# Causal pooling as banded TensorE products, and the decay levels spread over the tiles of the input projection

## The reference, cut to what matters

```python
def multiscale_pool(u, pool_w, pool_scale):
    c = jnp.cumsum(u32, axis=1)
    for g, w in enumerate(POOL_WINDOWS):          # 2, 4, 8, 16
        means.append((cg - lag) / cnt)            # trailing mean over w positions
    pooled = jnp.stack(means, axis=2) - u32
    y = jnp.einsum('bsgc,gcd->bsgd', pooled.astype(u.dtype), pool_w)
    return y.reshape(B, S, D_POOL) * pool_scale

def step(state, inp):                             # hgrn2_recurrence, one chunk
    b = jnp.cumsum(g_c, axis=2)
    o_inter = jnp.einsum('bhtd,bhdv->bhtv', q_c * jnp.exp(b), state)
    scores = jnp.einsum('bhtd,bhsd,bhtsd->bhts', q_c, k_c, decay)
    o_intra = jnp.einsum('bhts,bhsv->bhtv', scores, v_c)
    new_state = jnp.exp(b_last) * state + jnp.einsum('bhsd,bhsv->bhdv', k_dec, v_c)
```

## Time and profile before

| what | value |
|---|---|
| median of three executions | 2828.55 us |
| the profiled execution: its own time | 2831.76 us |
| the profiled execution: its span | 2830.0 us |
| PE busy | 2630.8 us, 93% |
| DVE busy | 1367.0 us, 48% |
| ACT busy | 727.9 us, 26% |
| POOL busy | 685.3 us, 24% |
| mean granted TensorE clock | 0.958 |

### The profile page before, as it was taken

How to read it: one execution, slowest core, us unless ns; L and a number is a source line. 1 busy time by engine, 2 the same in 40 slices (tenths; PEclk the granted TensorE clock), 3 DMA queues, 4 the chain that set the end, 5 groups by cost and what they waited for, 6 DMA issues and landing times. The chain is left out here.

```text
span 2830.0 us, 36447 instructions
## 1 busy us (share of the span) xinstructions
PE 2630.8 (93%) x13232; PEld 2086.7 (74%) x13232; DVE 1367.0 (48%) x2271; ACT 727.9 (26%) x1465; POOL 685.3 (24%) x422
## 2 busy tenths in 40 slices
PE   7989888989879999997799999899999987999997
PEld 4867756867648888876678888788888765788886
DVE  4356834367653334467653333533344575633344
ACT  2135621156431110042431110211110424311101
POOL 1000031000223331117243331233311163433311
PEclk9998989979989999999899999999999997999999
DMA  5310013300122333221122333133332220223332
GB/s 193 97 45 1 2 60 126 96 1 2 38 89 92 94 102 102 78 84 58 39 81 90 96 108 102 56 97 96 99 103 88 75 67 31 79 93 96 103 103 80
DMA packets 57268, 222.22 MB, mean 79 GB/s; under 512 B 6664, under 2 KB 7816, under 8 KB 56768
## 3 DMA queue, kind: packets, MB, share of 16 engines
q1 hardware_dynamic: 56000, 214.01, 23.7%
q10 hardware_dynamic: 1152, 6.68, 0.6%
HBM read 218.51 MB, written 2.15 MB: 78 GB/s over the span
## 5 line engine op out<-in xcount | busy, mean ns | idle before, releaser
L214 PE MATMUL bank<-xh,two_hi 128*128 128x512 f32 x1856 | 741.5, 400 | 37.7 <-ACT xh L1173 33.7
L215 PE MATMUL bank<-xh,two_lo 128*128 128x512 f32 x1856 | 737.8, 398 | 0.0
L217 PE MATMUL bank<-xl,two_hi 128*128 128x512 f32 x1856 | 727.0, 395 | 0.0
L167 DVE CAST two_hi<-two_raw 128x1024 fp32r<-128x1024 f32 (+1 forms) x292 | 228.3, 782 | 952.7 <-PE bank L217 950.7
L214 PEld LDWEIGHTS bank<-xh,two_hi 128*128 128x128 f32 x1856 | 352.5, 190 | 129.3 <-issue 36.6
L215 PEld LDWEIGHTS bank<-xh,two_lo 128*128 128x128 f32 x1856 | 352.8, 190 | 82.0 <-issue 0.5
L217 PEld LDWEIGHTS bank<-xl,two_hi 128*128 128x128 f32 x1856 | 351.0, 189 | 82.7
L169 DVE TENSOR_TENSOR two_lo<-two_raw,two_hi 128x1024 fp32r<-128x1024 f32 (+1 forms) x292 | 395.5, 1355 | 10.0
L1395 POOL TENSOR_TENSOR up_hm<-up_sg,up_hm 128x512 f32<-128x512 f32 x88 | 197.9, 2249 | 581.2 <-ACT up_hm L1377 581.2
L214 PE MATMUL bank<-hh,two_hi 128*128 128x512 f32 x704 | 276.3, 392 | 0.0
L217 PE MATMUL bank<-hl,two_hi 128*128 128x512 f32 x704 | 274.1, 389 | 0.0
(11 more groups left out here) (314 smaller groups left out, 3185.6 us busy)
## 6 DMA issues: line engine op xcount, KB each, us to landing
two_raw<-in_up SPq DMA_DIRECT2D x180, 512.0 KB, 3.6
two_raw<-in_down SPq DMA_DIRECT2D x64, 704.0 KB, 4.0
one_raw<-in_w_in SPq DMA_DIRECT2D x52, 512.0 KB, 3.6
two_raw<-in_w_in SPq DMA_DIRECT2D x40, 512.0 KB, 3.6
one_raw<-in_w_out SPq DMA_DIRECT2D x16, 512.0 KB, 3.6
two_raw<-in_w_out SPq DMA_DIRECT2D x16, 512.0 KB, 3.7
w<-in_w ACTq DMA_DIRECT2D x2, 2048.0 KB, 10.6
x<-in_x SPq DMA_DIRECT2D x1, 2048.0 KB, 8.3
```

Source lines behind the costliest of these rows:

```text
L167: v.tensor_copy(st.hi[:, h, 0:w], st.raw[:, r, 0:w]).then_inc(st.hi_made, 1)
L214: pe.matmul(out[:], wh, xh[:, kx, :], start=start, stop=False)
L215: pe.matmul(out[:], wl, xh[:, kx, :], start=False, stop=False)
L217: return pe.matmul(out[:], wh, xl[:, kx, :], start=False, stop=stop)
```

## The change

In the mixers the pooling leaves POOL. For each chunk of 128 tokens PE multiplies u by the pooling weights (`pool_weights`, 16 products of 128 columns), ACT copies the results to SBUF, and PE multiplies them by constant banded matrices `kb` that hold the window means minus one (`pool_steps`: per window four products of 128 columns and three of 16 columns for what spills over from the chunk before). `kb` is loaded anew in each layer by a DMA that the ACT queue issues at tile 8, 128 rows of 4352 bytes. ACT writes `xh` of the pooling straight from PSUM, DVE writes its `xl`.

DVE takes over from POOL the key product and the query product; the keys' decay is made by ACT in 16 activations. The decay chain, the level work, the value and key transposes, five of the six masked levels and the pooling's weight product are placed among the tiles of the projection. `LINE` is doubled from 32 to 64 numbers. Core of the diff:

```diff
-LINE = 32
+LINE = 64
...
+    MASKED_LEVELS = (2, 3, None, 4, 5, 6)
...
             if i == 8:
-                a.wait_ge(s["e3"], 1)
...
+                a.dma_start(kb[:], kit.d["kb"]).then_inc(s["steps"], 16)
+                a.wait_ge(s["b_made"], HH * NT)
+                for b in range(HH * NT):
+                    c = slice(b * P, (b + 1) * P)
+                    a.activation(kd[:, c], bb[:, c], ACT.Exp, scale=-1.0, bias=bb[:, b * P + P - 1:b * P + P]
+                                 ).then_inc(s["ke_exp"], 1)
+                a.activation(el[:], bb[:, P - 1:W:P], ACT.Exp).then_inc(s["ke_exp"], 1)
+                level_exps(0)
...
             if i == 17:
-                level_exps(3)
...
+                level_exps(6)
+                a.activation(qe, bb[:], ACT.Exp).then_inc(s["qe_exp"], 1)
+                a.wait_ge(s["z_mm"], NT)
+                for n in range(NT):
+                    a.activation(zt[:, n, :], bank[n][:], ACT.Copy).then_inc(s["z_kept"], 1)
...
+        for c in range(HH):
+            a.wait_ge(s["p_mm"], c + 1)
+            a.activation(kit.xh[:, c, :], bank[6 + c % 2][:], ACT.Copy, scale=kit.s2[:, Q_PS + c:Q_PS + c + 1]
+                         ).then_inc(s["hi_made"], 1)
...
     def vector(v):
...
-            if i == 10:
+            if i in (6, 7):
                 v.wait_ge(s["a_made"], 1)
-                for h in range(HH):
+                for h in ((0, 1) if i == 6 else (2, 3)):
...
+            if i == 19:
+                v.wait_ge(s["qe_exp"], 1)
+                v.tensor_tensor(qe, qe, q, ALU.mult).then_inc(s["qe_made"], 1)
+                accumulate(4)
+        accumulate(5)
...
+        for c in range(HH):
+            v.wait_ge(s["hi_made"], c + 1)
+            v.scalar_tensor_tensor(kit.xl[:, c, :], bank[6 + c % 2][:], kit.s2[:, Q_PS + c:Q_PS + c + 1],
+                                   kit.xh[:, c, :].bitcast(F32), ALU.mult, ALU.subtract).then_inc(s["lo_made"], 1)
...
     def tensor(pe):
...
+        for i in range(D_V, N_IN2):
             dense(i)
+            if i == 11:
+                top_level(0)
+            if i == 12:
+                top_level(1)
+                turn_values(0)
+                turn_values(1)
+            if i == 13:
+                turn_values(2)
+                turn_values(3)
+            if i == 14:
+                masked_level(0)
+            if i == 15:
+                masked_level(1)
+            if i == 16:
+                masked_level(2)
+                turn_keys()
+            if i == 17:
+                masked_level(3)
+                pool_weights()
+            if i == 18:
+                masked_level(4)
+        masked_level(5)
+
+        pe.wait_ge(s["z_kept"], NT)
         for n in range(NT - 1):
             for h in range(HH):
...
+        pe.wait_ge(s["steps"], 16)
+        pe.wait_ge(s["out_taken"], 2 + N_IN2)
+        for c in range(HH):
+            if c >= 2:
+                pe.wait_ge(s["lo_made"], c - 1)
+            pool_steps(c)
...
     def gpsimd(g):
         apply_gpsimd(g, kit, s)
-        g.wait_ge(s["b_made"], HH * NT)
         g.wait_ge(s["v_turned"], NT)
...
         g.memset(at[:, 0:2, :, :], 0.0).then_inc(s["zeroed"], 1)
         g.memset(at[:, 2:4, :, :], 0.0).then_inc(s["zeroed"], 1)
```

More of the change, by code:

```diff
@@ L1539, in mixers @@
     dense_banks = bank[6:8]
[L1540 to L1546, removed]
+    s = kit.sems("mix", DENSE + APPLY_SEMS + (
+        "chain_v", "abs_f", "exp_f", "ln_f", "ls_made", "km_made", "k_made", "a_made", "m_made", "lb_in", "lb_act", "lb_made",
+        "e2", "e3", "e4", "b_made", "sub_made", "exp_made", "top_mm", "ke_exp", "lv_made", "lev_mm", "acc_made", "at_made",
+        "v_turned", "v_kept", "qe_exp", "qe_made", "kd_made", "k_turned", "k_kept", "kv_mm", "st_made", "o_mm", "o_kept",
+        "osq_made", "o_summed", "oln_made", "orstd_made", "y_made", "g_made", "z_mm", "z_kept", "p_mm", "hi_made",
+        "lo_made", "ylo_made", "zeroed", "steps"))
     q = p2[:, D_Q:D_Q + HH, :].rearrange("p h t -> p (h t)")
@@ L1639, in scalar @@
[L1639 to L1647, removed]
@@ new lines, in scalar @@
+            if i == 16:
+                a.wait_ge(s["k_turned"], NT - 1)
+                for n in range(NT - 1):
+                    a.activation(kr[:, n, :, :], bank[n][:].rearrange("p (h c) -> p h c", h=HH), ACT.Copy
+                                 ).then_inc(s["k_kept"], 1)
+            if i == 17:
+                level_exps(6)
[3 more added lines that the diff above has]
+                    a.activation(zt[:, n, :], bank[n][:], ACT.Copy).then_inc(s["z_kept"], 1)
@@ L1843, in top_level, with masked_level @@
                 mm.then_inc(s["top_mm"], 1)
-        def masked_level(i):
-            if i < len(MASKED) - 1:
-                pe.wait_ge(s["lv_made"], 2 * (i + 3))
-            if i >= 2:
-                pe.wait_ge(s["acc_made"], 2 * i - 3)
+        def masked_level(j):
+            i = MASKED_LEVELS[j]
+            if i is not None:
+                pe.wait_ge(s["lv_made"], 2 * i + 2)
+            if j < 2:
+                pe.wait_ge(s["v_kept"], NT)
+            else:
+                pe.wait_ge(s["acc_made"], max(1, 2 * (j - 2)))
             for n in range(NT):
@@ new lines, in pool_weights, with pool_steps @@
+        def pool_weights():
+            pe.wait_ge(s["k_kept"], NT - 1)
+            pe.wait_ge(s["out_taken"], 2 + D_U + HH)
+            for n in range(NT):
+                for c in range(HH):
+                    mm = pe.matmul(bank[n][:, c * P:(c + 1) * P], p2[:, D_U + c, n * P:(n + 1) * P],
+                                   kit.s2[:, Q_PW + c * P:Q_PW + (c + 1) * P], start=True, stop=True)
+                mm.then_inc(s["z_mm"], 1)
+        def pool_steps(c):
+            out = bank[6 + c % 2]
+            for n in range(NT):
+                first = FIRST_STEP if n == 0 else INNER_STEP
+                mm = pe.matmul(out[:, n * P:(n + 1) * P], zt[:, n, c * P:(c + 1) * P], kb[:, c, first:first + P],
+                               start=True, stop=n == 0)
+                if n:
+                    mm = pe.matmul(out[:, n * P:n * P + PADT], zt[:, n - 1, c * P:(c + 1) * P],
+                                   kb[:, c, SPILL_STEP:SPILL_STEP + PADT], start=False, stop=True)
+            mm.then_inc(s["p_mm"], 1)
@@ L1879, in tensor @@
-        for i in range(D_U + 1, D_G):
-            dense(i)
-        pe.wait_ge(s["v_kept"], NT)
-        top_level(0)
-        dense(D_G)
-        dense(D_G + 1)
-        top_level(1)
-        dense(D_G + 2)
-        dense(D_G + 3)
-        for c in range(HH):
-            pool_product(c)
-        pe.wait_ge(s["p_kept"], HH)
-        masked_level(0)
-        masked_level(1)
-        pe.wait_ge(s["kd_made"], 1)
-        pe.wait_ge(s["out_taken"], 2 + N_IN2)
-        pe.wait_ge(s["at_made"], 3 * NT)
+        dense_products(pe, st, s["out_taken"], l, "w_in_2", DC, kit.xh, kit.xl, dense_banks, first=D_Q, last=D_V)
```

266 lines of the change are left out of this document (121 added, 145 removed).

## The result

Median of six executions each: 2828.88 us before (2825.17 to 2831.14), 2749.25 us after (2740.12 to 2758.69), ratio 0.9721 [0.9699, 0.9742], which is 79.6 us less. The forecast was 2785.0 in a range from 2742 to 2806. The direction was right and the range held the time, but the likeliest value was 36 us too high; the forecast's own range, 2775 to 2797, did not hold it either. The wider range did because its lower end was rival 1, and the result lies 7 us above that rival's 2742, which had a chance of 0.18.

The account below looks back on a forecast made before the run. PE was taken to bound the kernel, with losses in the mixer tails. Per layer 62.0 - 26.8 - 13.4 = 21.8 us, twice 43.6, padding nothing: 2828.55 - 43.6 = 2785 us; range 2742 to 2806, its own 2775 to 2797.

Parts of the forecast that it names:

- rival 1: Padding helps because weights and activations then lie alike in 128-byte halves: 2742 us, chance 0.18.
- What bounded the kernel: PE, busy in 93% of the span; the mixer tails of 62.0 and 61.9 us were where time could be saved.
- Work between tiles: Five masked levels, key transposes and pooling weight products added among projection tiles: 13.4 us a layer at full clock.
- Is anything late: DVE, ACT and the `kb` load meet PE's waits among the tiles; tightest is tile 8's split, 0.6 us to spare.
- sign of being wrong: PE waiting for `two_lo` or "issue" between tiles, or tile intervals far from the mixers moved by over 0.05 us.
- The new tail: Tile 19 to the first output-projection product: 26.8 us, bounds 20.5 to 30, with PE idle 6 us for DVE.
- the restart: PE's loss to the low clock behind its wait for DVE in the tail, taken as 2.3 us.
- Sum of the rearrangement: Old tail less new tail and work between tiles: 21.8 us saved a layer, 43.6 in both.
- The padding: LINE 64 moves tiles behind `eps` by 128 bytes against `xh`; taken as no effect, though bounded at -43 us.
- Rival 2: Padding hurts because the slow half itself costs and `hh` and stationary tiles move into it: 2853 us, chance 0.09.
- Rival 3: Masked levels among tiles stall through "issue" gaps or a late DVE, 9 us a layer: 2803 us, chance 0.15.
- Rival 4: Pooling leaves POOL but the tail then waits for DVE; already in the forecast, 2773 us if that work were hidden.

Follow-up runs that it names:

- a: The kernel after with LINE set back to 32, so the reordering of the mixers without the padding: 2784.21 us, ratio 0.9849.
- e: The kernel after with seven unread filler products on PE while it would wait for DVE in the tail: 2748.72 us, ratio 0.9739.
- g: The kernel after with four pooling banks instead of two and DVE's query product moved from tile 19 to 17: 2730.14 us, ratio 0.9677.
- c: The kernel after with 128 bytes put in front of `hh`, shifting it against the weight tiles: 2763.94 us, ratio 0.9779.
- b: The kernel before with only the padding (LINE 64): 2792.36 us, ratio 0.9876.
- l: The kernel after with two of the five masked levels placed among the tiles put back behind the last tile: 2752.05 us, ratio 0.9723.
- j: The kernel after, unchanged, run again: 2756.49 us, ratio 0.9738.
- f: The kernel after with the four pooling windows in four banks instead of two: 2736.03 us, ratio 0.9688.
- k: Repeat of the kernel after with four pooling banks and DVE's query product at tile 17: 2729.97 us, ratio 0.9643.

## Why the prediction was right or wrong

- **What bounded the kernel:** right. The tails were the place where the rearrangement saved its time.
- **Work between tiles,** forecast 13.4 us: measured 62.1 - 49.9 = 12.2 in a. A level lengthens a tile by 1.46 us in the kernel after (E(15) to E(16) is 6.90, a bare tile 5.44) where I had taken 1.7, the middle of two rows; five of them make the 1.2 us. Its 128 records take 1.30 of this, and the faster row, which ran at this clock, was the one to take. Key transposes (1.3) and pooling weights (3.6) came as forecast.
- **Is anything late:** right in substance. In the stretch from tile 11 to 19 PE is busy for 61.00 of 61.00 us. The margin of 0.6 us for the split of tile 8 did not exist: in DVE's timeline of the kernel after it ends at 1228.83, and ACT began its copy of tile 7, with which PE was done then, at 1228.74. PE waited 0.18 us for it (third row), the kind of wait that I had named as a sign of being wrong, but too small to matter. `kb` was never waited for.

```profile
1226.88 0.69 DVE L166 CAST two_hi<-two_raw 128x1024 fp32r<-128x1024 f32 x1
1227.60 1.23 DVE L168 TENSOR_TENSOR two_lo<-two_raw,two_hi 128x1024 fp32r<-128x1024 f32 x1
1228.88 0.50 PE L213 MATMUL bank<-xh,two_hi 128*128 128x512 f32 x1 [0.18 <-DVE two_lo L168]
```

- **The new tail,** forecast 26.8 us: 30.5 in a, 30.9 after. This is the step that failed within the rearrangement. The wait ends 13.1 us after tile 19 (forecast 12.6), and its cause is the queue on DVE that I had counted. Behind it I had 2.2 + 9.7 for the work; in e it takes 25.8 - 13.1 = 12.7, since a window of pool steps takes 1.5 us and not 1.1. The rest is the restart, taken as 2.3 and measured as 5.1. I carried it over from the output stage before, which took 1.9 more than its work. The windows of that tail (around the last masked level, then the first 4.5 us of the output stage) show what differs:

```profile
1366.90:1373.00 6.10, 2.64 (x257) 2.38 (x256) 5.75 (x14) 0.00 (x0) 3.12 (x3) 1.00 0.02 5
1375.50:1380.00 4.50, 4.44 (x21) 4.47 (x22) 0.37 (x1) 0.60 (x1) 0.00 (x0) 0.50 0.00 0
```

The clock was at 1.00 before PE's 4.0 us wait, fell in it, and was granted again after 4.4 us of work; behind the 5.9 us wait of the kernel after it took 10.9 us of work. So a restart has no fixed price, and why the low clock lasted more than twice as long here isn't shown by any run. Of the sum, then, the restart is the mis-sized term: + 2.8 for the restart, + 0.8 for the work, + 0.5 for the wait. The prediction's lower bound of 20.5 us was also wrong by its own terms, which add up to 6.6 + 2.2 + 9.7 = 18.5; g measured 20.0.
- **Sum of the rearrangement,** forecast 43.6: 38.6. The work between the tiles was 1.2 us a layer too dear in the forecast and the tail 3.7 too cheap (30.5 in a), so the errors partly cancel.
- **The padding,** taken as nothing: this was the step that failed. Of the 36 us by which the value was too high, the padding makes 29 in the second block, and 12 lie outside it, in part padding too (8 us by the estimate above) and in part scatter; the rearrangement takes 5 off. The bound I had written (6 ns for each of these products, -43 us) was right in sign and within a quarter per product (5.3 ns in the second block), and rival 1 named the mechanism that c shows, both operands alike. I chose zero because no row told address from width and data, and gave the gain 0.18. But the earlier trace rows had equal shapes at an equal clock 6 ns apart, so some condition did cost, and what the edit changed was one of three that could be it. About a third would have been the fair chance by those rows. The likeliest value may be zero then all the same, yet not at half of the whole.
- **A rule weighed there:** the Trainium skill, "SBUF — State Buffer", section "SBUF: two separate sides", has PE never waiting for its ports. By it the padding is worth nothing; a and b show 29 to 30 us. The measurement decides, and the rule can't be taken to mean that PE's rate is independent of where its operands lie.
- **Rival 2** (the slow half itself) is ruled out by b, where `hh` was moved into that half with the weights and kept its 392 ns, and by c, where only `hh` moved and became slow in the other half. **Rival 3** (stalls among tiles) did not occur; its gaps of "issue" are absent from the profiled execution of the kernel after and return in l. What they are is not shown. **Rival 4** was in the forecast and g shows its price: without the wait for DVE's queue the tail is 20.0, not 30.9.

## What to carry to other kernels

Let moving and stationary operands of fp32r products start at the same place within 256 bytes: it is one line of padding, and here 2 to 6 ns of some 230 on thousands of products. When a wait of PE is about to remain, count the restart beside the wait (5.9 + 5.1 us in this tail, of which some came back elsewhere, and 4.0 + 1.9 in the tail before), and look whether one more bank or one operation moved earlier on the queue behind it removes both. And before work is hidden among tiles, ask which engine bounds the tail it is taken from.

## What was not expected of the hardware

- 24 fp32r products of 512 columns take 5.44 us when the starts of their operands agree within 256 bytes, 5.60 when they are 128 bytes apart. From the second blocks: 2.2, 5.2 and 5.9 ns a product at 64, 128 and 32 bytes, without an order by distance.
- PE's "issue" gaps, 1.7 to 2.6 us each: two in l, where three levels follow each other (384 records), none in the profiled execution of after, where a tile of 5.4 us lies between the levels. They don't vanish wholly: inside a last level there are 0.7 us in j, the same kernel, and 0.4 to 1.0 in e, f, g and k. A level of 128 records in 1.30 us is 10 ns a record.
- After 5.9 us without work PE stayed at 1.2 GHz for 10.9 us although it was busy for 10.87 of them; in e, kept busy, it stayed at 2.4 GHz through the tail. In the kernel before, after 4.0 us without work, it stayed at 1.2 GHz for only 4.4 us of work.
